# Layer 1 value products of the prompt attention as rounded high and low parts

## The reference

```
logits = einsum('bqkgd,bskd->bkgqs', qg, k) * HEAD_DIM ** -0.5
logits = logits + (cq - ck)
p = softmax(where(causal, logits, -inf), axis=-1)
o = einsum('bkgqs,bskd->bqkgd', p, v)
```

## Time and profile before

| what | value |
|---|---|
| runs of the kernel | 1653.64, 1656.75, 1657.67 us (median 1656.75) |
| the profiled execution | 1655.06 us, its span 1653.2 us |
| TensorE busy | 1533.9 us, 93% of the span |
| VectorE busy | 746.5 us, 45% |
| ScalarE busy | 660.2 us, 40% |
| mean granted TensorE clock | 0.949 of 2.4 GHz |
| prompt attention of layer 1 | about 994 to 1146 us |
| one group of 16 units there | 36.1 us |

### The profile page before, as it was taken

One profiled execution on the slowest core, in us unless ns is written; L12 is line 12 of the kernel. 1 busy time (PEld: TensorE's weight loads), 2 busy tenths in 40 slices (PEclk: granted clock), 3 DMA queues, 4 the chain that ended last, 5 costly groups with the idle time before them and its releaser, 6 DMA issues.

```text
span 1653.2 us, 30349 instructions
## 1 busy us (share of the span) xinstructions
PE 1533.9 (93%) x12125; PEld 1385.4 (84%) x12125; DVE 746.5 (45%) x1515; ACT 660.2 (40%) x1217; POOL 191.8 (12%) x283
## 2 busy tenths in 40 slices
PE   6998879899798999999999789999798999999998
PEld 4884567786597999999999777887598999999998
DVE  1437967784336333333453622322446443344444
ACT  4424344454224333343433545654234333234333
POOL 0131521111010000000000331211010000000012
PEclk9799779999799999999999898999898999999999
DMA  9438630032623464554332140013722232322121
GB/s 287 133 108 270 206 108 26 1 127 103 212 95 102 129 200 135 172 172 132 120 105 87 33 141 27 27 77 126 254 80 69 86 101 76 101 84 82 59 88 52
DMA packets 154561, 189.90 MB, mean 115 GB/s; under 512 B 6806, under 2 KB 148414, under 8 KB 150167
## 3 DMA queue, kind: packets, MB, share of 16 engines
q1 hardware_dynamic: 144930, 147.90, 28.0%
q0 software_dynamic: 5600, 36.44, 5.8%
q10 hardware_dynamic: 3936, 4.24, 0.9%
HBM read 183.92 MB, written 4.83 MB: 114 GB/s over the span
## 4 chain that ended last, share of the span: by engine, by line
PE 80%; DVE 6%; issue 5%; ACT 3%; DMA 2%; POOL 2%; SPq 1%; ACTq 0%; DVEq 0%; POOLq 0%; PEldq 0%
PE ps L545 56%; PE ps L1290 4%; PE ps L1344 3%; PE ps L1366 3%; PE ps L571 2%; PE ps L1311 2%; PE ps L1357 1%; DMA ring<-in_w_ada 1%; PE ps L1596 1%; PE ps L1653 1%; PE ps L1317 1%; PE ps L582 1%; DVE wL L529 1%; DVE rt L681 1%; ACT wH L523 1%
## 5 line engine op out<-in xcount | busy, mean ns | idle before, releaser
L545 PE MATMUL ps<-hH,wH 128*128 128x260 f32 x2608 | 536.7, 287 | 37.2 <-DVE hL L723 14.8
L545 PE MATMUL ps<-hH,wL 128*128 128x260 f32 x2608 | 531.1, 286 | 0.0
L545 PE MATMUL ps<-hL,wH 128*128 128x260 f32 x2608 | 530.8, 286 | 0.0
L545 PEld LDWEIGHTS ps<-hH,wH 128*128 128x128 f32 x2608 | 408.3, 192 | 45.6 <-issue 34.0
L529 DVE TENSOR_TENSOR wL<-ring,wH 128x1024 fp32r<-128x1024 f32 (+1 forms) x168 | 200.2, 1193 | 531.4 <-ACT wH L523 525.1
L523 ACT ACTIVATE wH<-ring 128x1024 fp32r<-128x1024 f32 (+1 forms) x182 | 187.8, 1032 | 554.0 <-PE ps L545 532.9
L545 PEld LDWEIGHTS ps<-hH,wL 128*128 128x128 f32 x2608 | 408.0, 191 | 0.0
L545 PEld LDWEIGHTS ps<-hL,wH 128*128 128x128 f32 x2608 | 407.9, 191 | 0.0
L1434 ACT ACTIVATE arena<-arena 128x128 f32<-128x128 f32 (+3 forms) x128 | 72.1, 563 | 133.5 <-DVE arena L1539 133.3
L1366 PE MATMUL ps<-arena 128*128 128x64 f32 (+1 forms) x640 | 90.0, 273 | 15.2 <-ACT arena L1442 8.9
L1366 PEld LDWEIGHTS ps<-arena 128*128 128x128 f32 x640 | 83.4, 195 | 22.5 <-ACT arena L1442 13.1
(11 more groups left out here) (298 smaller groups left out, 1737.8 us busy)
## 6 DMA issues: line engine op xcount, KB each, us to landing
ring<-in_w_ada SPq DMA_DIRECT2D x48, 1024.0 KB, 8.5
ring<-in_w_up SPq DMA_DIRECT2D x44, 1024.0 KB, 5.1
ring<-in_w_down SPq DMA_DIRECT2D x16, 1024.0 KB, 5.6
ring<-in_w_in_a SPq DMA_DIRECT2D x8, 1024.0 KB, 6.8
ring<-in_w_down SPq DMA_DIRECT2D x8, 768.0 KB, 4.9
ring<-in_w_in_b SPq DMA_DIRECT2D x6, 1024.0 KB, 6.6
ring<-in_w_o_a SPq DMA_DIRECT2D x4, 1024.0 KB, 11.0
ring<-in_w_o_b SPq DMA_DIRECT2D x4, 1024.0 KB, 9.9
```

Source lines behind the costliest of these rows:

```text
L545: ins = pe.matmul(ps[:, 2 * p + half, 0:HT], w[:, h, kc, t * P:t * P + P], mov[:, k0 + kc, half * HT:half * HT + HT], start=(first and kc ...
```

## The change

For layer 1 alone, the probabilities and the values are each split in a high part, rounded to fp32r, and a low part, the remainder in fp32r.

- Values: once per layer ScalarE writes the high parts (128 x 1024) and VectorE the low ones into `VHL`, where each key block has for each group 64 high and 64 low columns side by side.
- Probabilities: ScalarE's copy out of PSUM now writes `PTH` (rounded). VectorE then subtracts it from the same PSUM buffer and writes `PTL`, one subtraction for each unit, and counts it in `at_lo`.
- Products: for each key block two products, stationary `PTH` and stationary `PTL`, each with 128 moving columns (high and low values). All four products of parts are summed, in two halves of 64 columns that belong to one head. PSUM buffer 4 holds 512 columns instead of 256.
- Order: the value product of unit v moves from TensorE's step v + 3 to step v + 4, ahead of the turn. It waits for `at_lo`. The turn of unit v waits for `at_lo` of unit v - 2 instead of `at_pt`.
- Outputs: VectorE first sums the two halves (a reduction of 512 elements to 256), then scales. `outputs` moves behind Sm in its step, and the subtraction of unit u - 3 follows it.

```diff
+            def split_values(v):
+                gv, qt, hh = g if v >= 0 else g - 1, v % NU // GR, v % GR
+                pe.wait_ge(S("at_lo"), (n - NKV) * NU + (v + 1))
+                if hh == 0 and (v >= GR or not first):
+                    pe.wait_ge(S("at_on"), n * QT + v // GR)
+                for kb in range(qt + 1):
+                    for part in (PTH, PTL):
+                        ins = pe.matmul(ps[:, 4, hh * P:hh * P + P], part[:, v % 2, kb * P:kb * P + P], VHL[:, kb, ds(gv * P, P)],
+                                        start=(kb == 0 and part is PTH), stop=(kb == qt and part is PTL))
+                ins.then_inc(S("at_o"), 1)
...
+                v = u - 4
+                if l == 1 and (v >= 0 or not first) and v < NU:
+                    split_values(v)
                 v = u - 2
...
-                        pe.wait_ge(S("at_pt"), n * NU + (v - 1))
+                        if l == 0:
+                            pe.wait_ge(S("at_pt"), n * NU + (v - 1))
+                        else:
+                            pe.wait_ge(S("at_lo"), (n - NKV) * NU + (v - 1))
...
-                if (v >= 0 or not first) and v < NU:
+                if l == 0 and (v >= 0 or not first) and v < NU:
...
-                act.activation(PT[:, v % 2, 0:w], ps[:, 2 + v % 2, 0:w], ACT.Copy).then_inc(S("at_pt"), 1)
+                act.activation((PT, PTH)[l][:, v % 2, 0:w], ps[:, 2 + v % 2, 0:w], ACT.Copy).then_inc(S("at_pt"), 1)
...
+                act.activation(high_values, values, ACT.Copy)
...
+                    parts = ps[:, 4, :].rearrange("p (h x d) -> p h d x", h=GR, x=2)
+                    dve.tensor_reduce(outs, parts, AX.X, ALU.add).then_inc(S("at_rl"), 1)
+                    dve.wait_ge(S("at_rl"), 2 * (n * QT + (qt + 1)) - NKV * QT)
+                    sums = outs
...
-                    if u % GR == GR - 1 and (u >= GR + 3 or not first):
+                    ends = u % GR == GR - 1 and (u >= GR + 3 or not first)
+                    if ends and (l == 0 or u >= NU):
                         outputs(n, u // GR - 1)
...
+                    if ends and l == 1 and u < NU:
+                        outputs(n, u // GR - 1)
+                    v = u - 3
+                    if l == 1 and (v >= 0 or not first) and v < NU:
+                        w = (v % NU // GR + 1) * P
+                        dve.wait_ge(S("at_pt"), n * NU + (v + 1))
+                        dve.tensor_tensor(PTL[:, v % 2, 0:w], ps[:, 2 + v % 2, 0:w], PTH[:, v % 2, 0:w].bitcast(F32), ALU.subtract)\
+                            .then_inc(S("at_lo"), 1)
...
+            if l == 1:
+                dve.tensor_tensor(low_values, values, high_values.bitcast(F32), ALU.subtract)
```

More of the change, by code:

```diff
@@ L249, in build @@
         A_N = 19900
+        arenaR, = shared(("arenaR", [P, A_N], F32R))
         arena = sb("arena", [P, A_N])
@@ L276, in build @@
         OT = part(KC * TOK).rearrange("p (k t) -> p k t", k=KC)
+        VHL = arenaR[:, at[0]:at[0] + QT * NKV * P].rearrange("p (t c) -> p t c", t=QT)
         mflat = part(QT * SEQ)
@@ L307, in build @@
         Pr = part(2 * SEQ).rearrange("p (b c) -> p b c", b=2)
+        PTH = arenaR[:, at[0]:at[0] + 2 * SEQ].rearrange("p (b c) -> p b c", b=2)
         PT = part(2 * SEQ).rearrange("p (b c) -> p b c", b=2)
@@ L312, in build @@
         rl = part(16)
+        PTL = arenaR[:, at[0]:at[0] + 2 * SEQ].rearrange("p (b c) -> p b c", b=2)
+        part(2 * SEQ)
         vmore = part(NPG * PC, work0)
@@ L1417, in to_qst @@
             copy(qst[0:HD, 2 * t + 1, :], raw2[HD:P, t, :]).then_inc(S("at_q"), 1)
+        values = Vt.rearrange("p t (g d) -> p t g d", g=NKV)
+        high_values = VHL.rearrange("p t (g d) -> p t g d", g=NKV)[:, :, :, 0:HD]
+        low_values = VHL.rearrange("p t (g d) -> p t g d", g=NKV)[:, :, :, HD:P]
         def act_attn(act, l):
@@ L1508, in outputs @@
                 dve.reciprocal(rl[:, c:c + GR], lsum[:, c:c + GR]).then_inc(S("at_rl"), 1)
-                dve.wait_ge(S("at_rl"), n * QT + (qt + 1))
-                dve.tensor_tensor(On[:, qt % 2, :].rearrange("p (h d) -> p h d", h=GR),
-                                  ps[:, 4, 0:PC].rearrange("p (h d) -> p h d", h=GR),
+                outs = On[:, qt % 2, :].rearrange("p (h d) -> p h d", h=GR)
+                sums = ps[:, 4, 0:PC].rearrange("p (h d) -> p h d", h=GR)
+                if l == 0:
+                    dve.wait_ge(S("at_rl"), n * QT + (qt + 1))
+                else:
+                    parts = ps[:, 4, :].rearrange("p (h x d) -> p h d x", h=GR, x=2)
+                    dve.tensor_reduce(outs, parts, AX.X, ALU.add).then_inc(S("at_rl"), 1)
+                    dve.wait_ge(S("at_rl"), 2 * (n * QT + (qt + 1)) - NKV * QT)
+                    sums = outs
+                dve.tensor_tensor(outs, sums,
                                   rl[:, c:c + GR].unsqueeze(2).to_broadcast([P, GR, HD]), ALU.mult)\
```

## The result

The changed kernel takes 1670.26 us (median of seven runs, 1663.97 to 1671.51), the kernel before 1655.99 us in its seven runs beside it. The ratio is 1.0088 with a 95% interval of 1.0075 to 1.0102: 14 to 15 us slower. Forecast were 1669.5 us and slower; as a difference, 12.8 us were forecast.

The account below looks back on a forecast made before the run. TensorE, busy 93% of the span, was taken as the bound. Boundaries 6.0, inside groups 3.9, end 2.8 and start 0.1 made 12.8 us on 1655.06, or 1669.5 us against the median; own range 1662 to 1683, whole range 1660 to 1706.

Parts of the forecast that it names:

- TensorE gains nothing: Layer 1's value products: 320 weight loads before and after, each pass bound by its load at 0.105 us; change 0.
- rival 1: Value products: narrow fp32r runs at the 32-bit rate, four cycles a column, 34 us over 320; 1703 us; chance 0.35.
- Rival 2: Value products: the new products' load is shorter, 0.055 us apart, 16 us gained on TensorE; 1657 us; chance 0.10.
- VectorE's prices: VectorE's added work: subtraction 0.29 to 0.69 us, reduction about 0.69, following product 0.43; busy time up about 43 us.
- A middle boundary: Between two groups of layer 1's attention: TensorE waits for VectorE's chain, 2.0 us more each, 6.0 for three.
- step 4: TensorE's step 4 inside a group: a wait of 0.1 us twice, and 0.5 in the last group.
- Step 8: TensorE's step 8 inside a group: it stands 0.8 us in three groups, and 0.6 in the last.
- first wait: At a middle boundary, TensorE stands 2.2 us until the subtraction of unit 12 is done.
- The end: From the last logits to the last output turn: a longer VectorE chain, 2.8 us more.
- step 12: TensorE's step 12 inside a group: no wait, as two projection parts cover it; 0.2 us in the last group.
- Rival 4: Waits bring TensorE's clock to 1.2 GHz: up to 5 us; chance 0.05, shared with anything between.
- The start: Start of layer 1's attention: writing the values' high and low parts falls mostly in ScalarE's covers; 0.1 us.

Follow-up runs that it names:

- products alone: Changed kernel without subtractions and reductions, in the old order, high part of the probabilities used twice: 1653.65 us, ratio 0.9998 to the kernel before.
- the filling: Changed kernel plus idle TensorE products in its two waits at a boundary between groups (ten, then six): 1663.85 us, ratio 1.0056 to the kernel before.
- filled start: Idle products in TensorE's waits at the start of layer 1's attention: kernel before 1652.23 us (0.9994); its plain products in the changed order 1646.26 us (0.9963).
- high part first: Changed kernel with each unit's high-part products all ahead of its low-part products, which alone wait for the subtraction: 1660.54 us, ratio 1.0033 to the kernel before.
- no reduction: Changed kernel without the reduction, outputs scaled straight from the high half of the columns: 1655.03 us, ratio 1.0005 to the kernel before.

## Why the prediction was right

The time came out 0.8 us above the forecast of 1669.5. As a difference it is 14.3 us against 12.8, since the kernel before had a median of 1655.99 in the seven runs and 1656.75 in the three that the forecast stood on. The mechanism, no gain on TensorE and waits for VectorE's chain, was right; that the number came so near is in part luck, as the points show:

- **TensorE gains nothing: right.** 320 loads, products about 0.105 to 0.117 us apart at 2.4 GHz, and 0.9998 for the products alone. The column count did not bind at 128 columns of fp32r, so rival 1 (0.35, 1703 us) did not happen. It was given a large chance for want of a row, and one kernel settled it.
- **Loads of fp32r are as slow as the others: right.** They take 193 ns in the mean with the products alone. Rival 2 (a shorter load) did not happen either.
- **VectorE's prices: right but for one.** 0.69 and 0.662 us measured, and the halves 64 columns apart cost nothing extra. Busy time rose by 38 us in all, where 43 were forecast. By rows 31.2 us of subtractions, 10.6 of reductions, 1.2 of low values and 2.3 of longer scaling products were added, 45.3 together; neighbouring instructions of VectorE overlap at their edges (the scaling product of 1069.64 lasts until 1070.07, the subtraction begins at 1069.99), and the page counts such time once. The term that was wrong is "the product that follows stays at 0.43": the reduction gives it a second input in SBUF, its mean is 0.57, and it took 1.58 to 2.59 us where it met GpSimd's subtraction.
- **A middle boundary, 2.0 us plus 0.1 at step 4: the waits right in place, the size by luck.** A gap of about 2 us ended by the subtraction, one under 1 us at step 8 and a group of some 39 us were the signs given; they are 1.67, 0.29 and 39.5 to 41.9. The first wait was forecast as 2.2 us and is 1.67, mainly since VectorE's instructions overlap a little (the chain from reciprocal to the end of the subtraction takes 1.82 us where the working had 2.1). The second was 1.0 and is 0.52 to 1.17 over the two traces. Step 8 was 0.8 and is 0.29. Against that, step 4 was 0.1 and is 1.38 at full clock. With the clock held by the filling, a group costs 3.5 us more than before (39.9 and 39.6 against 36.4 and 36.1) where the forecast had 2.9. For the third boundary the forecast comes to 3.1 us (2.0, and 0.5 and 0.6 for steps 4 and 8 of the last group); it cost 3.4 us with a fall of the clock and 1.8 without one.
- **The end, 2.8 us (3.0 with step 12 of the last group, which lies in the same stretch): right.** 2.4 measured.
- **Rival 4, the clock: wrong as it was put.** It had been given up to 5 us, under a chance of 0.05 with other mixtures, because no single wait is over 2.3 us. It happened around or behind a first wait of 1.45 to 1.68 us, at five of the six boundaries in the two traces of the changed kernel. The difference between the changed kernel and the filled one is 4.4 us over the three boundaries in the first trace (1.2, 2.3 and 0.9 from unrounded marks), and 6.7 us in the second. Since the filling itself costs 0.7 us at the third boundary, the price of the clock is somewhat higher; within the changed kernel the third group is 1.6 us longer with a fall of about 3 us than without.
- **The start, 0.1 us: nothing against it.** 35.1 before and after; with 33.4 to 35.8 in the other traces without a filled start, 0.1 us can't be told.

The sum by the marks of the first trace: waits 3.5 + 3.5 + 2.5 (0.7 of the last is the filling), end 2.4, clock 4.4, together 16.4 us before rounding; the profiled spans differ by 13.7, since this trace began the stage 2 us earlier by scatter. By the ratios, the kernel with the clock held is 9.3 us slower than the kernel before (7 to 11), and the clock makes 5.3 us more. The forecast had 12.8 us of waits and end, nearly whole by the marks (11.9) and too much by the ratios, and nothing for the clock. So the figure is right because two errors worked against each other: the waits were put too high in part (first wait, step 8), and the clock and the meeting of the scaling product with GpSimd (about 1.4 us at each of two boundaries) were left out.

What stays open: how much of the 9 us by which both additions together exceed the sum of the two alone is clock and how much is the chain. The filling gives the clock 4 to 7 us; the rest would be waits that add up only when subtraction and reduction stand in one chain, which is argued and not shown. Why the clock falls at two boundaries of three in one trace and at all three in another was not tried either. The size of the waits alone does not settle it: without the reduction it stayed at 1.00 behind two waits of 1.10 us each, and in the trace of the products alone it fell for about 3 us around 0.40 and 0.59 us.

## What to carry to other kernels

A product of 64 columns that is bound by its weight load does not get cheaper by being split into parts that need as many loads; look at what the load costs before counting columns. Where a step is put on an engine that is only half busy, follow the chain that the bottleneck waits for at the place where the bottleneck has nothing else to do: two additions that cost 3.6 and 4.6 us alone cost 17 together. And when TensorE gets new waits, look at the granted clock of the stretches behind them; the price of a wait can be paid again in the ten microseconds after it.

## What the runs showed of the hardware that I had not expected

- TensorE's clock fell to 1.2 GHz around or behind a single wait of 1.45 to 1.68 us at five of six boundaries, for about 3 to 14 us in which TensorE was busy but for the second wait; at one of the five it fell only behind the second wait (1.17 us). With idle products in the waits it stayed at 2.4 GHz in the one trace taken, as it did with waits of 0.96 and 0.53 us in the same places (high part first) and of 1.10 and 1.10 us (no reduction). It fell once around waits of 0.40 and 0.59 us (products alone).
- A VectorE product with both inputs in SBUF took 1.58 to 2.59 us instead of 0.43 while GpSimd's subtraction on SBUF ran, and ended 0.29 us behind it. With one input in PSUM it took 0.43 inside the same subtraction.
- 128 moving columns of fp32r are hidden behind a weight load of 128 columns: 0.105 to 0.117 us a product, as for 64 columns of plain 32-bit data in a pass, and 0.9998 of the time for the whole kernel.
